# A hybrid decoder step on one core: the order of work in the softmax of the prompt's latent attention

## The chip, the cores and the metric

The kernel runs on one core of one Trainium2 chip. The metric is the device time of one execution in microseconds (us). The kernel before took 5193.56 us, the median of 3 runs (5190.1 to 5200.91).

## The reference, cut to what matters

One step of a one-layer decoder for a prompt of 512 tokens and a sample group of 8 x 4 tokens, which share the weights: a recurrent branch, multi-head latent attention (MLA) and attention into memory tokens, merged; then a PEER expert layer. The change touches only the MLA of the prompt, 16 heads, causal:

```python
q = jnp.einsum('bsc,chd->bshd', rmsnorm(qa, g_q_a), w_q_b)
q_nope, q_pe = q[..., :NOPE_DIM], rope(q[..., NOPE_DIM:], q_pos)     # 128 and 64 wide
ckv_new = rmsnorm(kva[..., :KV_LORA], g_kv_a)                        # 256 wide
krope_new = rope(kva[..., KV_LORA:], q_pos)
# per block of 128 queries, per head:
s = (q_abs . ckv + q_pe . kpe) * (NOPE_DIM + ROPE_DIM) ** -0.5
s = jnp.where(k_pos <= pos, s, -inf)
o = softmax(s) @ ckv            # then the value half of w_kv_b
```

All data are float32.

## The kernel before

One program of five engines' instruction streams, ordered by hand; engines wait for each other's semaphores with constant or loop-dependent counts. There is no planner for this part. The prompt's projections come first, then the memory attention, then the prompt's MLA, the sample's MLA over its gathered pages, the merges, and PEER, which takes most of the time.

The prompt's MLA is a loop of 4 with two rounds inside (L722 to L784 on TensorE, L1158 to L1184 on ScalarE, L1501 to L1537 on VectorE). A round `n` does two heads, `e` = 0 and 1. It has these steps:

- TensorE makes three query products of 4 x 2 matmuls each (`cols`, L571; into the bank pairs 0/1, 2/3 and 6/7; the first has the nope part of one head, the second that of the other, the third the rotary part of both), then the keys of both heads (L737, banks 0 and 1), the swapped rotary part (L571), the values (L744, banks 2 and 3), and the sample's absorbed queries (L749, bank 4). ScalarE copies query, key and value products out of PSUM (L1165, L1167, L1168); VectorE applies the rotation (L1508 to L1511).
- The softmax part goes in steps `u`, one for each block of 128 queries of each head, 8 in all; block `t` = `u % 4` has `(t + 1) * 128` keys. Scores (L763, L764) go to bank `u % 3`. VectorE adds the causal mask (L1529) and takes the negative maximum (L1470, L1471). ScalarE takes the exponential and its sum into `pbuf` (L1127). VectorE normalises (L1474, L1475). TensorE transposes the probabilities in blocks of 128 (L774) into bank 5 or 6, ScalarE copies them to `pT` (L1183), and after the fourth block of a head TensorE multiplies with the values into bank 7 (PV, L782), which VectorE copies to `omla` (L1537, semaphore `mla_out`).
- TensorE transposes step `u - 2` after the scores of step `u`: a lag of two. ScalarE's stream has the same lag: exp of `u`, then the copy of `u - 2`. VectorE normalises with a lag of one.
- `spin(bank, n)` (L566) issues `n` fillers: matmuls of a matrix of ones with 512 columns of `hT`, into a bank that nobody reads. Two stand ahead of the softmax part, one ahead of each of the first six transposes, two ahead of each of the last two, and one ahead of each PV product.
- Before the three query products of a round TensorE waits until VectorE has stored the last output of the round before (`mla_out`, L728).

In the trace one float32 matmul is two records. SP loads the weights of a round into two of the five slots of a ring as these come free. When the last round's weight slots are free, GpSimd begins to gather the pages of the first sample sequence (L488 to L498, 16 gathers), which the sample's MLA needs.

Of the kernel before, what the change touches and what calls it, by code (L numbers as in the profile page):

```python
# [25 lines left out]
P = 128  # L26
# [3 lines left out]
SEQ = 512  # L30
NB = 8
NS = 4
SAMP = NB * NS
T = SEQ + SAMP
# [3 lines left out]
ROPE = 64  # L38
# [38 lines left out]
NSCR = 7032  # L77
# [100 lines left out]
def build(nc, A, O):  # L178
    with ExitStack() as ctx:
# [83 lines left out]
        qabs = region(X0 + 4 * T + 1024, 2, NB, 64)  # L263
        assert X0 + 4 * T + 2048 <= OMLA
        vv = region(S0, 4, 256)
        pbuf = region(S0 + 1024, 3, SEQ)
        pT = region(S0 + 1024 + 1536, 4, SEQ)
        qpe = region(S0 + 1024 + 1536 + 2048, NB, 64)[0:ROPE]
        ropt = region(S0 + 1024 + 1536 + 2048 + 512, T)
        assert S0 + 1024 + 1536 + 2048 + 512 + T <= SCR + NSCR  # L270

        qs2 = [region(X0, 3, 64), region(X0 + 2560, 3, 64)]
        ob = region(X0 + 2752, 256)[0:64]
# [279 lines left out]
        def _(pe):  # L553
# [169 lines left out]
            with pe.Fori(0, 4) as i:  # L723
                for e2 in range(2):
                    wa = use("mla", 2 * e2, i)
                    wb = use("mla", 2 * e2 + 1, i)
                    n = i * 2 + e2
                    pe.wait_ge(s("mla_out"), i * 4 + 2 * e2 + 1)  # L728
                    for m in range(3):
                        for k in range(4):  # L730
                            last = cols(pair((0, 1, 3)[m]), wa[:, (4 * m + k) * P:(4 * m + k + 1) * P], proj[:, QA + k, :],
                                        k == 0, k == 3)
                        last.then_inc(s("q_ready"), 1)
# [19 lines left out]
                    spin(5, 2)  # L753
                    pe.wait_ge(s("kv_stored"), n * 2 + 2)
                    pe.wait_ge(s("q_turned"), n * 3 + 3)
                    for u in range(8 + 2):
                        if u < 8:
                            e, t = u // 4, u % 4
                            if u >= 3:
                                pe.wait_ge(s("mla_exp"), n * 8 + u - 2)  # L760
                            bank = u % 3
                            w_ = (t + 1) * P
                            mm(psum[:, bank, 0:w_], qn[:, e, t * P:(t + 1) * P], kn[:, e, 0:w_], start=True, stop=False)  # L763
                            mm(psum[:, bank, 0:w_], qp[64 * e:64 * e + 64, t * P:(t + 1) * P],  # L764
                               proj[64 * e:64 * e + 64, KROPE, 0:w_], start=False, stop=True).then_inc(s("mla_scores"), 1)
                        if u >= 2:
                            q = u - 2
                            e, t = q // 4, q % 4
                            spin(4, 1 if u < 8 else 2)
                            pe.wait_ge(s("mla_probs"), n * 8 + q + 1)  # L770
                            if q >= 2:
                                pe.wait_ge(s("mla_pT"), n * 8 + q - 1)
                            for j in range(t + 1):
                                last = nc.tensor.transpose(psum[:, 5 + q % 2, j * P:(j + 1) * P], pbuf[:, q % 3, j * P:(j + 1) * P], ident)  # L774
                            last.then_inc(s("mla_turned"), 1)
                            if t == 3:
                                spin(4, 1)
                                pe.wait_ge(s("mla_pT"), n * 8 + q + 1)
                                if e == 1:
                                    pe.wait_ge(s("mla_out"), n * 2 + 2)  # L780
                                for j in range(4):
                                    last = mm(psum[:, 7, j * P:SEQ], vv[:, j, e * P:(e + 1) * P], pT[:, j, j * P:SEQ],  # L782
                                              start=(j == 0), stop=(j == 3), skip_group_check=True)
                                last.then_inc(s("mla_pv"), 1)  # L784
# [224 lines left out]
        def _(act):  # L1009
# [148 lines left out]
            with act.Fori(0, 4) as i:  # L1158
                for e2 in range(2):
# [6 lines left out]
                    act.wait_ge(s("kv_ready"), n + 1)  # L1166
                    a_(kn, psum[:, 0:2, :], ACT.Copy).then_inc(s("kv_stored"), 1)  # L1167
                    a_(vv.rearrange("p (a b) n -> p a (b n)", a=2), psum[:, 2:4, :], ACT.Copy).then_inc(s("kv_stored"), 1)  # L1168
                    for u in range(8 + 2):
                        if u < 8:  # L1170
                            t = u % 4
                            act.wait_ge(s("mla_max"), n * 8 + u + 1)
                            if u >= 3:
                                act.wait_ge(s("mla_turned"), n * 8 + u - 2)
                            exp(pbuf[:, u % 3, 0:(t + 1) * P], psum[:, u % 3, 0:(t + 1) * P], v("nm", u % 4, 1), MLA_SCALE,
                                v("sum", u % 4, 1), s("mla_exp"))
                        if u >= 2:
                            q = u - 2
                            t = q % 4
                            act.wait_ge(s("mla_turned"), n * 8 + q + 1)  # L1180
                            if q == 4:
# [143 lines left out]
        def _(dve):  # L1325
# [177 lines left out]
            with dve.Fori(0, 4) as i:  # L1503
                own.enter(i, 2 * (8 + 8 + 8) + 2 * 1)
                for e2 in range(2):
# [18 lines left out]
                    for u in range(9):  # L1524
                        if u < 8:
                            e, t = u // 4, u % 4
                            dve.wait_ge(s("mla_scores"), n * 8 + u + 1)
                            bank = psum[:, u % 3, :]
                            do(V.tensor_tensor(bank[:, t * P:(t + 1) * P], bank[:, t * P:(t + 1) * P], causal, ALU.add))  # L1529
                            neg_max(bank[:, 0:(t + 1) * P], v("nm", u % 4, 1), MLA_SCALE, s("mla_max"))  # L1530
                        if u >= 1:
                            q = u - 1
                            dve.wait_ge(s("mla_exp"), n * 8 + q + 1)
                            normalise(pbuf[:, q % 3, 0:(q % 4 + 1) * P], v("rc", q % 4, 1), v("sum", q % 4, 1), s("mla_probs"))
                    for e in range(2):
                        dve.wait_ge(s("mla_pv"), n * 2 + e + 1)
                        V.tensor_copy(omla[:, ds(i * 4 + e2 * 2 + e, 1), 0:SEQ].squeeze(1), psum[:, 7, :]).then_inc(s("mla_out"), 1)  # L1537
# [472 lines left out]
```

## Time and profile before

| | |
|---|---|
| time, median of 3 | 5193.56 us |
| the profiled execution's own time | 5196.23 us |
| its span | 5194.4 us |
| mean granted TensorE clock | 0.889 |
| TensorE matmul busy | 4054.4 us (78%) |
| VectorE busy | 2797.3 us (54%) |
| GpSimd busy | 1426.3 us (27%) |
| ScalarE busy | 382.5 us (7%) |
| chain that ended last | PE 49%, DMA 23%, DVE 13%, issue 8%, POOL 7%, ACT 1% |
| the filler line L566 in the chain | 2% of the span |

How to read it: the span is that of one profiled execution, from its first to its last instruction. PE is TensorE, PEld its weight loads, DVE VectorE, ACT ScalarE, POOL GpSimd, SP SyncE. The busy share is an average over stages with different limits; which engine bounds the stretch of the change is read from the rows of that stretch. The chain follows back from the last instruction, at each step to what released it.

### The profile page before, as it was taken

Reading aid. Unit: us, or ns where it says so; the run is one execution under the profiler, and the core shown is the slowest. Engines: PE = TensorE matmul, PEld = TensorE weight load, DVE = VectorE, ACT = ScalarE, POOL = GpSimd, SP = SyncE. Lnnn points to the kernel's source line nnn. Section 1 sums busy time; section 2 is a strip of 40 time slices with the busy share of each in tenths; the row PEclk is TensorE's granted clock in tenths of the full one; section 3 lists DMA queues with packets and bytes.
Section 4 is the critical chain, followed back from the end, with each engine's and each line's share of the span. In section 5 each row is a group of like instructions: output and inputs, shape, how many; then the busy total and the mean of one; then the engine's idle time right before and its main releaser. Section 6 shows DMA issues by size and latency. Waiting matters only on the chain.

```text
span 5194.4 us, 39086 instructions
## 1 busy us (share of the span) xinstructions
PE 4054.4 (78%) x14526; PEld 2447.8 (47%) x14526; DVE 2797.3 (54%) x3638; ACT 382.5 (7%) x826; POOL 1426.3 (27%) x1257
## 2 busy tenths in 40 slices
PE   9999999998899999999899796999999990000000
PEld 7888665553389938555555344544443330000000
DVE  3235022321100004777777575688876645699998
ACT  1022012221000001000000001000000000000000
POOL 0000100013400001344455443212122217777533
PEclk9999989999989999999999898999999995555555
DMA  4211520113566645888899996699999987799999
GB/s 156 70 68 65 177 102 25 36 40 122 162 221 243 242 159 198 353 347 355 361 411 412 370 393 264 251 384 393 375 400 419 419 338 249 271 406 410 417 422 377
DMA packets 234203, 1413.25 MB, mean 272 GB/s; under 512 B 34704, under 2 KB 35536, under 8 KB 86416
## 3 DMA queue, kind: packets, MB, share of 16 engines
q0 software_dynamic: 138960, 916.70, 44.9%
q1 hardware_dynamic: 81984, 458.79, 23.5%
q10 hardware_dynamic: 13088, 35.50, 1.8%
q8 instruction: 106, 1.74, 0.1%
q14 instruction: 65, 0.53, 0.0%
HBM read 1385.08 MB, written 25.75 MB: 272 GB/s over the span
## 4 chain that ended last, share of the span: by engine, by line
PE 49%; DMA 23%; DVE 13%; issue 8%; POOL 7%; ACT 1%; DVEq 0%; ACTq 0%; POOLq 0%; another core or an unknown queue 0%
PE psum L571 11%; PE psum L997 10%; DMA arena<-in_v,arena 9%; DMA arena<-in_u_cols 7%; PE psum L866 7%; DVE psum L1865 7%; DMA arena<-in_u,arena 6%; PE psum L975 3%; POOL arena L528 3%; PE psum L566 2%; POOL arena L546 2%; PE psum L905 2%; POOL arena L496 2%; PE psum L928 1%; DVE arena L1755 1%
## 5 line engine op out<-in xcount | busy, mean ns | idle before, releaser
L866 PE MATMUL psum<-arena 128*128 128x160 f32 (+1 forms) x5120 | 1190.0, 396 | 34.2 <-DVE arena L1598 33.4
L1865 DVE SCALAR_TENSOR_TENSOR psum<-arena,psum 128x2048 f32<-128x2048 f32 x381 | 897.4, 2355 | 285.4 <-DMA arena<-in_v,arena 245.9
L866 PEld LDWEIGHTS psum<-arena 128*128 128x128 f32 x5120 | 842.0, 192 | 381.7 <-issue 48.4
L997 PE MATMUL psum<-arena 128*128 128x512 f32 x2048 | 912.0, 599 | 32.9 <-DMA arena<-in_u_cols 28.5
L528 POOL DMA_INDIRECT arena<-in_v,arena x544 | 642.2, 1180 | 840.7 <-DVE psum L1865 362.4
L528 POOL DMA_INDIRECT arena<-in_u,arena x288 | 384.7, 1336 | 1485.7 <-DVE arena L1686 656.5
L997 PEld LDWEIGHTS psum<-arena 128*128 128x128 f32 x2048 | 379.3, 190 | 564.9 <-issue 421.7
L571 PE MATMUL psum<-arena 128*128 128x272 f32 x2432 | 561.6, 393 | 8.4 <-DVE arena L1537 6.5
L571 PEld LDWEIGHTS psum<-arena 128*128 128x128 f32 x2432 | 462.3, 190 | 105.1 <-DVE arena L1537 7.8
L1755 DVE SCALAR_TENSOR_TENSOR arena<-arena,pages 128x2048 f32<-128x2048 f32 x128 | 301.1, 2353 | 102.9 <-DMA arena<-in_v,arena 99.3
L1720 DVE CUSTOM_DVE_ANT_0 arena<-arena 128x2048 f32<-128x2048 f32 x128 | 291.3, 2293 | 87.4 <-DMA arena<-in_u,arena 86.7
L1837 DVE CUSTOM_DVE_ANT_0 arena<-arena,psum 128x2048 f32<-128x2048 f32 x128 | 288.4, 2285 | 88.2 <-DMA arena<-in_u,arena 87.5
L546 POOL DMA_INDIRECT arena<-products,arena x256 | 246.7, 964 | 137.8 <-issue 136.9
L489 POOL COPY stage_idx<-pages 128x16 uint32 x8 | 1.6, 195 | 724.2 <-PE psum L749 587.8
L566 PE MATMUL psum<-arena,ones 128*128 128x512 f32 (+1 forms) x416 | 197.4, 592 | 0.0
L952 PE MATMUL psum<-arena 128*128 128x512 f32 x384 | 167.4, 599 | 35.4 <-DVE arena L1598 35.4
L975 PE MATMUL psum<-arena 128*128 128x384 f32 x512 | 167.7, 486 | 1.0 <-ACT arena L1281 1.0
L483 POOL TENSOR_TENSOR arena<-arena 128x544 f32<-128x544 f32 x16 | 21.7, 1393 | 511.1 <-PE psum L571 511.1
L1365 DVE TENSOR_TENSOR arena<-psum,arena 128x544 f32<-128x544 f32 x31 | 22.5, 724 | 252.4 <-PE psum L571 251.7
L1470 DVE TENSOR_REDUCE vec<-psum 128x1 f32<-128x128 f32 (+2 forms) x88 | 41.6, 473 | 186.5 <-PE psum L669 179.5
L952 PEld LDWEIGHTS psum<-arena 128*128 128x128 f32 x384 | 73.8, 193 | 128.8 <-issue 92.8
L496 POOL DMA_INDIRECT arena<-in_pool_rows,stage_idx x128 | 121.8, 952 | 45.2 <-issue 38.3
(276 smaller groups left out, 3033.7 us busy)
## 6 DMA issues: line engine op xcount, KB each, us to landing
arena<-in_w_merge SPq DMA_DIRECT2D x160, 1024.0 KB
arena<-in_u_cols SPq DMA_DIRECT2D x256, 512.0 KB
arena<-in_w_out SPq DMA_DIRECT2D x32, 1024.0 KB
arena<-in_w_query SPq DMA_DIRECT2D x32, 1024.0 KB
arena<-in_w_proj SPq DMA_DIRECT2D x31, 1024.0 KB, 4.9
products<-arena ACTq DMA_DIRECT2D x32, 512.0 KB, 12.3
arena<-in_v,arena POOLq DMA_INDIRECT x544
arena<-in_w_mem_k SPq DMA_DIRECT2D x8, 1024.0 KB, 6.2
```

Of the source, the lines that this page charges most:

```text
L528: pool.indirect_dma_start(row, None, A[table], bass.IndirectOffsetOnAxis(ap=idx[:, r:r + 1], axis=0))\
L546: pool.indirect_dma_start(dense_acts[:, e:e + 1], None, products, bass.IndirectOffsetOnAxis(ap=elem_idx[:, e // 128, e % 128:e % 128 + 1], ...
L566: mm(psum[:, bank, 512 - width:512], ones[:, :], hT[:, 0, 0:width], start=True, stop=True)
L571: last = mm(out[:, a, :], w, rhs[:, a * HALF:(a + 1) * HALF], start=start, stop=stop)
L866: last = mm(out, w[:, (off + k) * P:(off + k + 1) * P], src[:, k0 + k, lo:hi], start=(k == 0), stop=(k == n - 1))
L952: last = mm(psum[:, 3 * (n % 2) + t, :], merged_b[:, 4 * q + k, t * P:(t + 1) * P], w[:, k, :], start=(q == 0 and k == 0), stop=(q == 3 an ...
L975: last = mm(psum[:, u % 2, 0:B_N], w[:, k * P:(k + 1) * P], hfT_b[:, k, :], start=(k == 0), stop=(k == KD - 1))
L997: last = mm(psum[:, 4 + DENSE * (b % 2) + t, :], hfT_b[:, k0 + k, t * P:(t + 1) * P], u_tiles[n % 4][:, k, :], start=(k0 + k == 0), stop=( ...
L1720: V.tensor_tensor_reduce(row, row, h, 1.0, 0.0, ALU.mult, ALU.add, out).then_inc(s("rows_used"), 1)
L1755: V.scalar_tensor_tensor(lone, row, atmp_3[:, r:r + 1], lone, ALU.mult, ALU.add).then_inc(s("rows_used"), 1)
L1837: V.tensor_tensor_reduce(four(row), four(row), acc[0], 1.0, 0.0, ALU.mult, ALU.add, acts_2[:, r:r + 1]).then_inc(s("rows_used"), 1)
L1865: V.scalar_tensor_tensor(a, four(row), atmp_b[:, t, r:r + 1], a if r else four(x1_b[:, t, :]), ALU.mult, ALU.add).then_inc(s("rows_used"), 1)
```

## The change

Scores rotate over four banks instead of three, `pbuf` has four buffers instead of three, and the lag between scores and transposes is three steps on TensorE and ScalarE. The waits that guard the rotation move by one accordingly. Fillers stand only ahead of the last three transposes, one each, and, as before, ahead of PV and of the softmax part. TensorE's wait for the last output of the round before stands ahead of the third query product instead of the first. `qpe` and `ropt` and `pT` get other addresses in the same memory. VectorE's lag is the same. The core of the diff:

```diff
-        pbuf = region(S0 + 1024, 3, SEQ)
-        pT = region(S0 + 1024 + 1536, 4, SEQ)
-        qpe = region(S0 + 1024 + 1536 + 2048, NB, 64)[0:ROPE]
-        ropt = region(S0 + 1024 + 1536 + 2048 + 512, T)
+        pbuf = region(S0 + 1024, 4, SEQ)
+        pT = region(S0 + 1024 + 2048, 4, SEQ)
+        qpe = region(X0 + 4 * T + 2048, NB, 64)[0:ROPE]
+        ropt = region(S0 + 1024 + 2048 + 2048, T)
...
-                    pe.wait_ge(s("mla_out"), i * 4 + 2 * e2 + 1)
                     for m in range(3):
+                        if m == 2:
+                            pe.wait_ge(s("mla_out"), i * 4 + 2 * e2 + 1)
...
-                    for u in range(8 + 2):
+                    for u in range(8 + 3):
                         if u < 8:
                             e, t = u // 4, u % 4
-                            if u >= 3:
-                                pe.wait_ge(s("mla_exp"), n * 8 + u - 2)
-                            bank = u % 3
+                            if u >= 4:
+                                pe.wait_ge(s("mla_exp"), n * 8 + u - 3)
+                            bank = u % 4
...
-                        if u >= 2:
-                            q = u - 2
+                        if u >= 3:
+                            q = u - 3
                             e, t = q // 4, q % 4
-                            spin(4, 1 if u < 8 else 2)
+                            if u >= 8:
+                                spin(4, 1)
                             pe.wait_ge(s("mla_probs"), n * 8 + q + 1)
...
-                    for u in range(8 + 2):
+                    for u in range(8 + 3):
                         if u < 8:
                             t = u % 4
                             act.wait_ge(s("mla_max"), n * 8 + u + 1)
-                            if u >= 3:
-                                act.wait_ge(s("mla_turned"), n * 8 + u - 2)
+                            if u >= 4:
+                                act.wait_ge(s("mla_turned"), n * 8 + u - 3)
...
-                        if u >= 2:
-                            q = u - 2
+                        if u >= 3:
+                            q = u - 3
```

## Rows read from the trace of the kernel before

**Rows 1.** The chain that ended last, 700 to 1200 us, shares by line.

```profile
by line: PE psum L566 22.9%; PE psum L571 19.8%; PE psum L764 9.4%; PE psum L782 7.6%; PE psum L763 7.5%; PE psum L744 5.5%; PE psum L737 5.5%; PE psum L774 3.5%; issue 3.0%; PE psum L714 2.6%; PE psum L811 1.5%; PE psum L705 1.5%; PE psum 
```

**Rows 2.** Windows: length, busy us (instructions) of each engine, granted clock, DMA share, GB/s.

```profile
895.00:946.00 51.00, 50.44 (x180) 29.83 (x180) 15.29 (x52) 11.77 (x29) 0.00 (x0) 1.00 0.09 31
1101.00:1163.00 62.00, 52.13 (x180) 30.45 (x180) 15.40 (x51) 11.82 (x29) 15.64 (x17) 0.92 0.28 85
```

**Rows 3.** Waits of TensorE from 792 to 1100 us: us in total, times, longest.

```profile
PE psum L571 <- DVE arena L1537: 5.6, 6, 0.9
```

**Rows 4.** Timeline, TensorE, one round: start, us, line, shapes, records, idle before.

```profile
916.88 0.38 PE L763 MATMUL psum<-arena 128*128 128x128 f32 x2
...
917.61 0.70 PE L763 MATMUL psum<-arena 128*128 128x256 f32 x2
...
918.87 0.91 PE L763 MATMUL psum<-arena 128*128 128x384 f32 x2
...
920.55 1.12 PE L566 MATMUL psum<-arena,ones 128*128 128x512 f32 x2
921.51 0.27 PE L774 MATMUL psum<-cst,arena 128*128 128x128 f32 x1
921.62 1.02 PE L763 MATMUL psum<-arena 128*128 128x512 f32 x2
...
923.63 1.12 PE L566 MATMUL psum<-arena,ones 128*128 128x512 f32 x2
...
930.25 2.41 PE L782 MATMUL psum<-arena 128*128 128x512 f32 x8
932.49 0.81 PE L763 MATMUL psum<-arena 128*128 128x384 f32 x2
...
938.33 1.88 PE L566 MATMUL psum<-arena,ones 128*128 128x512 f32 x4
940.05 0.49 PE L774 MATMUL psum<-cst,arena 128*128 128x128 f32 x3
...
943.40 2.41 PE L782 MATMUL psum<-arena 128*128 128x512 f32 x8
946.74 11.27 PE L571 MATMUL psum<-arena 128*128 128x272 f32 x48 [0.93 <-DVE arena L1537]
```

**Rows 5.** The same round's timeline, VectorE.

```profile
920.03 0.29 DVE L1475 TENSOR_SCALAR arena<-arena,vec 128x128 f32<-128x128 f32 x1
920.66 0.30 DVE L1529 TENSOR_TENSOR psum<-psum,cst 128x128 f32<-128x128 f32 x1 [0.34 <-PE psum L764]
...
921.85 0.35 DVE L1475 TENSOR_SCALAR arena<-arena,vec 128x256 f32<-128x256 f32 x1
923.74 0.30 DVE L1529 TENSOR_TENSOR psum<-psum,cst 128x128 f32<-128x128 f32 x1 [1.54 <-PE psum L764]
...
925.06 0.42 DVE L1475 TENSOR_SCALAR arena<-arena,vec 128x384 f32<-128x384 f32 x1
```

**Rows 6.** The same round's timeline, ScalarE.

```profile
924.99 0.69 ACT L1127 ACTIVATE arena<-psum,vec 128x512 f32<-128x512 f32 x1 [2.37 <-DVE vec L1471]
...
929.58 0.60 ACT L1183 ACTIVATE arena<-psum 128x512 f32<-128x512 f32 x1
```

**Rows 7.** Timeline of the last round, each of the three engines' stall.

```profile
1139.25 0.30 DVE L1529 TENSOR_TENSOR psum<-psum,cst 128x128 f32<-128x128 f32 x1 [6.71 <-remote]
...
1144.88 0.60 ACT L1183 ACTIVATE arena<-psum 128x512 f32<-128x512 f32 x1 [4.08 <-remote]
...
1145.53 4.08 PE L782 MATMUL psum<-arena 128*128 128x512 f32 x8 [9.64 <-ACT arena L1183]
```

**Rows 8.** Windows elsewhere in the kernel.

```profile
1205.00:1210.00 5.00, 3.09 (x8) 0.65 (x6) 1.22 (x1) 0.00 (x0) 3.78 (x5) 1.00 0.84 259
...
710.00:715.00 5.00, 5.00 (x27) 2.94 (x27) 1.03 (x5) 0.56 (x2) 0.00 (x0) 0.50 0.00 0
```

**Rows 9.** Timeline, TensorE, ahead of 710 us.

```profile
706.33 4.75 PE L714 MATMUL psum<-arena 128*128 128x4 f32 x32
```

More of the change, by code:

```diff
@@ L265, in build @@
         vv = region(S0, 4, 256)
-        pbuf = region(S0 + 1024, 3, SEQ)
-        pT = region(S0 + 1024 + 1536, 4, SEQ)
-        qpe = region(S0 + 1024 + 1536 + 2048, NB, 64)[0:ROPE]
-        ropt = region(S0 + 1024 + 1536 + 2048 + 512, T)
-        assert S0 + 1024 + 1536 + 2048 + 512 + T <= SCR + NSCR
+        pbuf = region(S0 + 1024, 4, SEQ)
+        pT = region(S0 + 1024 + 2048, 4, SEQ)
+        qpe = region(X0 + 4 * T + 2048, NB, 64)[0:ROPE]
+        ropt = region(S0 + 1024 + 2048 + 2048, T)
+        assert S0 + 1024 + 2048 + 2048 + T <= SCR + NSCR and X0 + 4 * T + 2048 + 512 <= OMLA
         qs2 = [region(X0, 3, 64), region(X0 + 2560, 3, 64)]
@@ L773, in _ @@
                             for j in range(t + 1):
-                                last = nc.tensor.transpose(psum[:, 5 + q % 2, j * P:(j + 1) * P], pbuf[:, q % 3, j * P:(j + 1) * P], ident)
+                                last = nc.tensor.transpose(psum[:, 5 + q % 2, j * P:(j + 1) * P], pbuf[:, q % 4, j * P:(j + 1) * P], ident)
                             last.then_inc(s("mla_turned"), 1)
@@ L1172, in _ @@
                             act.wait_ge(s("mla_max"), n * 8 + u + 1)
-                            if u >= 3:
-                                act.wait_ge(s("mla_turned"), n * 8 + u - 2)
-                            exp(pbuf[:, u % 3, 0:(t + 1) * P], psum[:, u % 3, 0:(t + 1) * P], v("nm", u % 4, 1), MLA_SCALE,
+                            if u >= 4:
+                                act.wait_ge(s("mla_turned"), n * 8 + u - 3)
+                            exp(pbuf[:, u % 4, 0:(t + 1) * P], psum[:, u % 4, 0:(t + 1) * P], v("nm", u % 4, 1), MLA_SCALE,
                                 v("sum", u % 4, 1), s("mla_exp"))
-                        if u >= 2:
-                            q = u - 2
+                        if u >= 3:
+                            q = u - 3
                             t = q % 4
@@ L1527, in _ @@
                             dve.wait_ge(s("mla_scores"), n * 8 + u + 1)
-                            bank = psum[:, u % 3, :]
+                            bank = psum[:, u % 4, :]
                             do(V.tensor_tensor(bank[:, t * P:(t + 1) * P], bank[:, t * P:(t + 1) * P], causal, ALU.add))
@@ L1533, in _ @@
                             dve.wait_ge(s("mla_exp"), n * 8 + q + 1)
-                            normalise(pbuf[:, q % 3, 0:(q % 4 + 1) * P], v("rc", q % 4, 1), v("sum", q % 4, 1), s("mla_probs"))
+                            normalise(pbuf[:, q % 4, 0:(q % 4 + 1) * P], v("rc", q % 4, 1), v("sum", q % 4, 1), s("mla_probs"))
                     for e in range(2):
```

## The prediction, made before the change was run

> **What bounds the kernel now.** I read the chain of waits over the stretch around the change first. The chain from 700 to 1200 us lies on TensorE almost throughout, and its largest line is L566, the filler matmuls, with 22.9% [rows 1]. In this stretch the chain runs through work whose result nobody reads.
>
> The windows say the same. The eight rounds of the prompt's MLA end at about 1163 us. A round takes 51 us, its TensorE time is 50.44 us of 51.00, VectorE has 15.29 and ScalarE 11.77, DMA is at 0.09, and the granted clock is 1.00 [rows 2]. So a microsecond taken off TensorE in a round is a microsecond off the kernel, as long as no wait takes its place. Everything after MLA starts on MLA's results (the sample's attention, then merges and PEER, whose weight loads begin only after the sample's last result), so I count the rest as shifted, not changed. The last round is another case: 62 us, with one TensorE wait of 9.64 us [rows 2, 7].
>
> The list of waits gives TensorE one regular wait in the rounds: 0.9 us, once a round, for VectorE's copy at L1537, six of them in the six rounds seen [rows 3]. The timeline of one round (rows 4; all full rounds have this pattern) shows where the time goes: its softmax part runs from 916.88 to the end of the last PV product at 945.8 (943.40 + 2.41), 28.8 us without a TensorE gap; the next round begins at 946.74; the other 22 us of a round are query, key and value products.
>
> **Part 1, the fillers.** Before, one filler stands ahead of each of the first six transposes and two ahead of each of the last two, ten in all, and one more ahead of each PV product. After, there is one ahead of each of the last three transposes, and the two ahead of PV stay. Removed: 10 - 3 = 7 a round. One filler is two matmul records. Two fillers take 1.72 us (938.33 to 940.05), so one is 0.86 us; after a score product it takes 0.96 us (920.55 to 921.51), and I count those 0.10 us as the score product's tail that stays [rows 4]. 7 x 0.86 = 6.02 us a round off TensorE's own work.
>
> **Part 2, the lag: what is late next.** The fillers gave ScalarE and VectorE time; now the third step of lag and the fourth bank must. I place the new order on a line with 0 at the first score product, with durations from rows 4 to 6. Scores 0 and 1 take 2.0 us together (916.88 to 918.87; 0.73 and 1.26), score 2 1.68 and score 3 2.01 us (921.62 to 923.63), a transpose 0.11 us a block of 128 (921.51 to 921.62), a PV product 2.24 us (930.25 to 932.49) [rows 4]. VectorE's step 2 lasts 1.54 us (920.66 to 922.20), step 3 1.74 us (923.74 to 925.48), and ScalarE's exp starts 1.25 us into it (924.99); the smaller ones take some 1.3 to 1.4 [rows 5]. ScalarE's exp of 512 takes 0.69 us, to which I add 0.1 for the read-out of its sum, its copy of 512 turned probabilities 0.60 us; smaller ones go down to about half [rows 6].
>
> - Scores 0 to 3 end at 5.7 without a gap. Probabilities 0 were ready 3.4 us after the first score's start (920.03 + 0.29 [rows 5]), so transpose 0 doesn't wait. Score 4 needs exp 0 (2.2): no wait.
> - Score 4, transpose 1, score 5, transpose 2, score 6, transpose 3 follow at 6.6, 6.8, 8.0, 8.5, 10.1, 10.6. VectorE goes through its steps 3, 4, 5 as they come and has probabilities 2 at 7.4 and 3 at 8.8: in time, with 0.7 us or more to spare. The copy of turned block 0 now stands behind exp 3 and ends at 7.9, transpose 2 wants its bank at 8.1: just in time.
> - The filler ends at 11.5. PV needs the copy of turned block 3, and in ScalarE's new order this stands behind exp 6, not exp 5. Score 6 ends at 10.1, its maximum is there at 11.3, exp 6 ends at 12.0, the copy at 12.6. **TensorE waits 1.1 us here.** This is the one real new wait.
> - PV, score 7 (end at 16.9), transpose 4, filler, transpose 5, filler: 19.0. Transpose 6 wants the bank of turned block 4, whose copy stands behind exp 7 (ends 19.0), so it starts at about 19.3: 0.25 us more. Transpose 7 and the last filler end at 21.7, the last copy at 21.6; the output of the first head must have been copied out of bank 7, which VectorE does after normalisation 7, at about 20.4. No wait. PV ends at 24.0.
>
> Laid out the same way, the order of before ends at 28.8, as the trace has it. So the softmax part goes from 28.8 to 24.0: 6.0 us removed, 1.35 given back, **4.7 us** a round. Bounds: 6.0 if the two waits cost nothing; 3.0 if they are twice as long and every transpose also waits a little (eight times 0.2 us: the distance from the end of a score to VectorE's start is 0.1 us, 923.63 to 923.74 [rows 4, 5]).
>
> **Part 3, the wait at the third query product.** It removes the 0.93 us in front of each round's first product [rows 3, 4]. The first two products take a third of 11.27 us each [rows 4], write banks 0 to 3, and by then VectorE's copy (0.69 us) is long over, so the moved wait costs nothing. Queued behind it are the third product and the key products; nothing comes late. ScalarE still waits for the same copy before it stores the first product, which ends 3.7 us in. Seven boundaries between eight rounds: 7 x 0.93 = **6.5 us**. The wait after the last round stays.
>
> **Part 4, buffers.** A fourth pbuf and other addresses for pbuf, pT, qpe and ropt change neither count nor size of any instruction, nor a DMA. Cost 0; I take 1 us to either side for what an address could do, about a hundredth of VectorE's 8 x 15.29 us [rows 2].
>
> **Part 5, the last round.** Its stall comes while GpSimd issues sixteen page gathers, begun when the round's last weight tile is free; VectorE shows 6.71 us and ScalarE 4.08 us idle before instructions whose inputs were there, released by something that the trace can't name, and TensorE waits 9.64 us and runs the next PV at half clock (4.08 us against 2.41) [rows 4, 7]. The gathers start at the same place of the round after the change, so I let VectorE come free at the same point, 1139.25 on the old scale, and ScalarE at 1144.9. In the new order exp 6 and copy 3 follow that: PV at 1146.5 instead of 1145.53. On the line above, 12.6 to 24.0 is 11.4 us from there, and a PV at half clock adds 1.9: the round ends at 1159.8, where it now ends at 1162.8. The last round gains **3 us**; bounds 0 (ScalarE's stall moves behind exp 6) and 15 (no stall: 4.7 and the 10.6 us by which this round is longer than the others).
>
> **Sum.** 7 x 4.7 + 6.5 + 3 = 42.4 us, against the profiled execution's 5196.2 us (span 5194.4 and 1.8 around it): 5153.8 us. That execution lies 2.7 us above the median of 5193.6; I state the prediction from the median: 5193.6 - 42.4 = **5151 us**. Ends of the terms: 7 x 3.0 + 6.5 + 0 = 27.5 (5166) and 7 x 6.0 + 6.5 + 15 = 63.5 (5130).
>
> **The clock, weighed.** TensorE is now 3% idle in a round where it had been full. In the trace the clock stays at 1.00 in 1205 to 1210 us with 3.09 of 5 us busy, so an idle microsecond does not lower it at once. But it was at 0.50 in 710 to 715 us with TensorE busy 5.00 of 5 us [rows 8], behind 32 matmuls of 4 columns [rows 9]: busy time alone doesn't hold the clock, and the fillers are 512 columns wide. For this kernel the first argument weighs more, because the scores, transposes and PV that remain are 128 to 512 columns wide. The Trainium skill (TensorE: Matmul & The Clock Gate, "A second HAM failure mode: psum-queue depth-cycling") says that short idle times between groups of matmuls, in a kernel that cycles through PSUM banks, can be enough for the clock to swing between its two levels. By that rule this change, more cycling and less filler, would be a loss; the trace of before has no such swing in the rounds.
>
> **Rivals.**
> - *The clock gives way* (the other side). Place: the softmax part of each round. Its TensorE work after the change is some 22.5 us a round at 2.4 GHz and would be twice that at 1.2 GHz (PV: 4.08 against 2.41 as recorded). Over 8 rounds a share f of it at the lower level costs 180 x f. It decides from f = 42/180 = 0.24; with f a third, 60 us: 5211 us; with all of it 5331 us. For it: rows 8 and 9. Against it: 1.00 in the rounds, the 22 us of dense products in each, and that scores 0 to 2 run without filler already, at full clock. Chance 0.09.
> - *Waits take the fillers' place.* Each step still lasts what ScalarE and VectorE need, and only part 3 and a few tenths a round stay: 5193.6 - 6.5 - 8 x 1.5 = 5175 us, or 5187 with nothing in the softmax. Against it: VectorE and ScalarE together are busy 27 of 51 us, and probabilities were ready over 1 us before their transposes. Chance 0.08, of which 0.04 within 0.2%.
> - *The last round's stall goes or halves*, because the stretch in which it falls is shorter or differently ordered: 6 to 12 us more than the sum, 5139 to 5145 us. The cause of the stall isn't in the rows. Chance 0.10.
> - *The forecast*, 27 to 50 us gained: 0.73.
>
> **How the numbers follow.** About 0.2%, 10 us, is what a measurement of this kernel tells from no change. Faster by more: 0.73 + 0.10 + 0.04 = 0.87; within: 0.04; slower: 0.09. The range goes from 5137, into the case without a stall, to 5169, just beyond the lower end of the terms, and leaves out the clock case and most of the waits' case.
>
> **What would show it.** The record of L566 in the rounds drops from 28 records to 14; TensorE's wait for L1537 at L571 is gone; a new TensorE wait of about 1 us for ScalarE's L1183 ahead of the first PV of each round; the round's period goes from 51.4 to 45.7 us; granted clock 1.00 in the full rounds; the stretch after MLA as long as before. A granted clock under 0.9 in the rounds, or TensorE waits ahead of most transposes, would make the prediction wrong.

## The result, and the profile after

The changed kernel takes 5144.24 us, the median of 4 runs (5135.76 to 5147.55); the kernel before took 5191.83 us (4 runs, 5187.19 to 5200.91). The ratio is 0.9904, 95% interval [0.9885, 0.9923]: 50 us faster, give or take 10. The forecast was 5151 us, 42.4 us less than before; it is right in sign and, for the full rounds, in mechanism.

The chain of the same stretch, 700 to 1200 us, by line:

```profile
by line: PE psum L571 19.7%; PE psum L765 9.1%; issue 8.5%; PE psum L784 7.9%; PE psum L764 7.7%; PE psum L566 7.0%; PE psum L745 5.5%; PE psum L738 5.5%; POOL arena L496 4.7%; PE psum L776 3.1%; PE psum L714 2.4%; PE psum L813 2.2%; DVE ve
```

The fillers (L566) have gone from 22.9% [rows 1] to 7.0%; query and key products (L571) now lead. The page gathers (POOL L496, 4.7%) and most of the larger share of "issue" (8.5%, was 3.0%) don't come from the full rounds: MLA ends 46 us earlier here, so the same stretch reaches 46 us further into the sample's MLA, and the last round's stall (below) holds one piece of 8 us. In the six full rounds alone "issue" is 3.0% of the chain and was 0.2%; that part belongs to the two new waits.

Windows of a full round and of the last (length, busy us of each engine with its instructions, granted clock, DMA share, GB/s):

```profile
876.00:921.00 45.00, 43.86 (x165) 26.60 (x164) 15.47 (x51) 11.60 (x29) 0.00 (x0) 1.00 0.11 35
1058.00:1117.00 59.00, 46.96 (x167) 28.22 (x166) 15.70 (x52) 11.82 (x29) 15.64 (x17) 0.88 0.29 89
```

Against [rows 2] the full round has lost 6 us, and its clock, the share of the full 2.4 GHz that TensorE was granted, is still 1.00; TensorE is busy 43.86 of 45 us. Its waits in six full rounds (us in total, times, longest):

```profile
PE psum L784 <- ACT arena L1185: 5.5, 6, 0.9
PE psum L776 <- ACT arena L1185: 1.1, 6, 0.2
```

The wait of [rows 3] is gone, and the two that the prediction named are there, once a round each, for ScalarE's copy L1185 (L1183 before). One full round on TensorE (start, us, line, shapes, records, idle before):

```profile
897.44 0.38 PE L764 MATMUL psum<-arena 128*128 128x128 f32 x2
...
907.60 0.66 PE L776 MATMUL psum<-cst,arena 128*128 128x128 f32 x4
908.09 1.02 PE L566 MATMUL psum<-arena,ones 128*128 128x512 f32 x2
910.03 2.42 PE L784 MATMUL psum<-arena 128*128 128x512 f32 x8 [0.92 <-ACT arena L1185]
912.29 1.02 PE L764 MATMUL psum<-arena 128*128 128x512 f32 x2
...
915.54 1.02 PE L566 MATMUL psum<-arena,ones 128*128 128x512 f32 x2
916.74 0.52 PE L776 MATMUL psum<-cst,arena 128*128 128x128 f32 x3 [0.18 <-ACT arena L1185]
...
918.39 1.02 PE L566 MATMUL psum<-arena,ones 128*128 128x512 f32 x2
919.25 2.41 PE L784 MATMUL psum<-arena 128*128 128x512 f32 x8
921.50 3.83 PE L571 MATMUL psum<-arena 128*128 128x272 f32 x16
```

The softmax part begins at 897.44 and its last PV at 919.25: 21.81 us, where it was 26.52 (916.88 to 943.40 [rows 4]), 4.71 us less. The filler ahead of the first PV starts at 908.09 and would be done 0.86 us later, at 908.95; PV starts at 910.03: 1.08 us of wait (the list counts 0.92, from the filler's modelled end). ScalarE shows why: the copy that PV needs stands behind the exp of step 6.

```profile
908.82 0.58 ACT L1129 ACTIVATE arena<-psum,vec 128x384 f32<-128x384 f32 x1 [0.61 <-DVE vec L1473]
...
909.39 0.59 ACT L1185 ACTIVATE arena<-psum 128x512 f32<-128x512 f32 x1
```

Ahead of transpose 6 it is 916.74 - (915.54 + 0.86) = 0.34 us. And the next round's products begin 2.25 us after the last PV's start (921.50), not 3.34 (943.40 to 946.74 [rows 4]). The round's period, from first product to first product, is 45.48 us (876.02 to 921.50) and was 51.37 (895.37 to 946.74), 5.89 us less.

The last round's stall is in this execution too, on VectorE, ScalarE and TensorE:

```profile
1099.83 0.30 DVE L1531 TENSOR_TENSOR psum<-psum,cst 128x128 f32<-128x128 f32 x1 [10.30 <-remote]
```

```profile
1092.80 0.49 ACT L1185 ACTIVATE arena<-psum 128x384 f32<-128x384 f32 x1 [3.06 <-remote]
...
1101.99 0.60 ACT L1185 ACTIVATE arena<-psum 128x512 f32<-128x512 f32 x1 [0.38 <-remote]
```

```profile
1102.64 4.63 PE L784 MATMUL psum<-arena 128*128 128x512 f32 x8 [11.62 <-ACT arena L1185]
...
1114.40 2.41 PE L784 MATMUL psum<-arena 128*128 128x512 f32 x8
```

VectorE stands for 10.30 us, ScalarE for 3.06 us at one copy, TensorE for 11.62 us, and again the next PV runs at half clock (4.63 us, where the second PV takes 2.41). "remote" means that the trace doesn't name the releaser. The round takes 59.81 us instead of 62.84.

### The profile page after: what moved, and what is told of

The parts are those of the page before. It is cut to its first block, busy times and chain, and to the rows that moved or that the text cites. A ratio compares the mean times of both kernels' runs of the same rounds, so it can differ in the third digit from the quotient of the medians.

```text
span 5134.0 us, 38854 instructions
## 1 busy us (share of the span) xinstructions
PE 3999.1 (78%) x14414; PEld 2424.2 (47%) x14414; DVE 2795.3 (54%) x3638; ACT 381.6 (7%) x826; POOL 1442.6 (28%) x1257
## 4 chain that ended last, share of the span: by engine, by line
PE 47%; DMA 24%; DVE 10%; issue 9%; POOL 9%; ACT 1%; ACTq 0%; DVEq 0%; POOLq 0%; another core or an unknown queue 0%
PE psum L571 11%; PE psum L999 10%; DMA arena<-in_v,arena 9%; DMA arena<-in_u_cols 8%; PE psum L868 7%; DMA arena<-in_u,arena 6%; POOL arena L528 4%; DVE psum L1867 4%; PE psum L977 3%; POOL arena L546 3%; PE psum L907 2%; POOL arena L496 2%; PE psum L930 1%; DVE arena L1757 1%; DVE arena L1722 1%
## 5 line engine op out<-in xcount | busy, mean ns | idle before, releaser
L528 POOL DMA_INDIRECT arena<-in_u,arena x288 | 403.8, 1402 | 1459.9 <-DVE arena L1688 656.2
L571 PE MATMUL psum<-arena 128*128 128x272 f32 x2432 | 562.5, 394 | 1.8 <-DVE arena L1501 0.9
L571 PEld LDWEIGHTS psum<-arena 128*128 128x128 f32 x2432 | 463.4, 191 | 97.7 <-issue 2.2
L566 PE MATMUL psum<-arena,ones 128*128 128x512 f32 (+1 forms) x304 | 135.6, 567 | 0.0
L496 POOL DMA_INDIRECT arena<-in_pool_rows,stage_idx x128 | 121.9, 952 | 45.2 <-issue 38.3
```

The source lines that it names most:

```text
L496: pool.indirect_dma_start(page_buf[:, pg, :], None, A["pool_rows"], bass.IndirectOffsetOnAxis(ap=stage_idx[:, pg:pg + 1], axis=0))\
L528: pool.indirect_dma_start(row, None, A[table], bass.IndirectOffsetOnAxis(ap=idx[:, r:r + 1], axis=0))\
L571: last = mm(out[:, a, :], w, rhs[:, a * HALF:(a + 1) * HALF], start=start, stop=stop)
```

## The experiments

A table first. "Full round" is the period of rounds 2 to 7, "MLA" the stretch from the first query product to the first instruction after the last round, "rest" what comes behind it. Times are medians; the kernel before was run again beside each group.

| kernel | time, ratio to before [95%] | full round | last round | MLA | rest |
|---|---|---|---|---|---|
| before | 5191.8 | 51.37 | 62.84 | 423.8 | 4030.7 |
| before, again | 5173.5 (one run) | 51.37 | 51.37 | 412.6 | 4022.1 |
| changed | 5144.2, 0.9904 [0.9885, 0.9923] | 45.48 | 59.81 | 381.2 | 4016.3 |
| changed, again | 5142.7 (one run) | 45.48 | 46.57 | 366.5 | 4034.7 |
| e1 wait only | 5171.9, 0.998 [0.9967, 0.9993] | 50.18 | 51.27 | 405.3 | 4027.3 |
| e2 fillers only | 5144.1, 0.9932 [0.991, 0.9954] | 46.87 | 49.22 | 381.0 | 4019.2 |
| e3 lag only | 5182.6, 1.0005 [0.9995, 1.0015] | 51.56 | 51.56 | 414.1 | 4025.2 |
| e4 copy first | 5115.6, 0.9879 [0.9855, 0.9903] | 43.93 | 45.02 | 355.5 | 4020.9 |
| e5 no filler | 5205.1, 1.0002 [0.9986, 1.0018] | 47.91 to 54.56 | 62.62 | 440.7 | 4027.7 |
| e6 gathers after the round | 5147.4, 0.9918 [0.9895, 0.9941] | 45.48 | 46.56 | 366.7 | 4034.1 |
| e7 gathers at the first PV | 5134.9, 0.9888 [0.9868, 0.9908] | 45.48 | 46.57 | 366.7 | 4028.9 |
| e8 e4 and e7 | 5124.9, 0.9865 [0.9841, 0.9889] | 43.93 | 45.02 | 355.3 | 4025.3 |
| e9 copy first, fewer fillers | 5122.5, 0.9889 [0.9871, 0.9908] | 43.60 to 44.97 | 45.98 | 360.5 | 4026.3 |
| e10 no filler in the softmax | 5152.9, 0.9954 [0.9939, 0.9968] | 47.38 to 48.11 | 48.48 | 386.0 | 4023.8 |

One thing has to be read from it before anything else: "rest" runs the same instructions in all of them and differs by up to 18 us between single executions, and by 18 us between two of the same kernel. A whole time can't settle a microsecond; the period of a full round can: it repeats to 0.01 us in every kernel but e5, e9 and e10 (and in e2 one of the full rounds, the second, took 49.20), where the clock fell within rounds, as is shown below.

**e1, the wait alone.** The kernel before with

```diff
-                    pe.wait_ge(s("mla_out"), i * 4 + 2 * e2 + 1)
                     for m in range(3):
+                        if m == 2:
+                            pe.wait_ge(s("mla_out"), i * 4 + 2 * e2 + 1)
```

> The kernel before with only the wait for the last output moved to the third query product. My theory (the gain is TensorE's own work and its one regular wait, step by step): the 0.93 us in front of each round's first product goes, the period of a full round falls from 51.37 to 50.44 us, the softmax part stays at 28.8 us, the time falls by 6.5 us. Rival (the wait was cover for something, ScalarE's stores say): the 0.93 us turns up again ahead of the key products, the period stays at 51.4, no change.

Measured: period 50.18 us, 1.19 less, not 0.93; the whole time is 10 us less (by the interval 4 to 17), where 6.5 were expected. The timeline of TensorE:

```profile
889.97 2.41 PE L783 MATMUL psum<-arena 128*128 128x512 f32 x8
892.22 11.16 PE L571 MATMUL psum<-arena 128*128 128x272 f32 x48
```

From the last PV's start the products now begin after 2.25 us instead of 3.34, 1.09 less, and the 48 product records take 11.16 where they took 11.27. The trace's idle of 0.93 us counts from the modelled end of the last matmul; the time until the next one could start, had it been free, begins 0.16 us earlier, and a stream that starts behind an idle engine takes 0.1 us longer. The rival, that the wait turns up elsewhere, is out.

**e2, the fillers alone.** The kernel before, lag and banks as they were:

```diff
-                            spin(4, 1 if u < 8 else 2)
+                            if q >= 5:
+                                spin(4, 1)
```

> The kernel before with the same seven fillers a round taken out, at the old lag of two, three banks and three pbufs, old wait. Theory A (TensorE's own work sets the round; the lag matters little): laid out with the same durations, new waits are 0.75 us for probabilities 2 and 0.86 us for the copy ahead of the first PV, the softmax part goes from 28.8 to 24.4 us and the period from 51.4 to 47.0; 31 us in seven rounds, about 3 in the last: 5158 us where before has 5192. Rival B (the third step of lag and the fourth bank are what makes the fillers removable): every transpose waits for its probabilities, the period stays at 49 or above and the gain under 18 us, or the clock falls in the softmax part.

Measured: period 46.87 us, 4.50 less, 5144.1 us, by the ratio 35 us less than before, where 34 were expected. Waits of TensorE in four full rounds:

```profile
PE psum L571 <- DVE arena L1538: 3.7, 4, 0.9
PE psum L775 <- DVE arena L1476: 3.3, 4, 0.8
PE psum L783 <- ACT arena L1184: 2.7, 4, 0.7
```

Beside the old wait at L571 they are the two forecast ones, for probabilities (0.8 a round) and ahead of the first PV (0.7), and nothing else. Rival B fails on the period and the gain: the fillers come out at the old lag. But in one point it is half right, the clock. In two of the eight rounds, the second (49.20 us) and the last (49.22), the clock fell right behind the wait for probabilities; in the second round:

```profile
817.55 0.55 PE L775 MATMUL psum<-cst,arena 128*128 128x128 f32 x3 [0.82 <-DVE arena L1476]
```

```profile
816.00:818.00 2.00, 1.18 (x9) 0.87 (x9) 1.86 (x7) 1.00 (x3) 0.00 (x0) 1.00 0.00 0
818.00:820.00 2.00, 2.00 (x5) 0.71 (x4) 0.73 (x4) 0.89 (x4) 0.00 (x0) 0.50 0.00 0
820.00:823.00 3.00, 3.00 (x8) 1.87 (x8) 1.24 (x5) 1.05 (x3) 0.00 (x0) 0.50 0.00 0
```

Each such fall costs about 2.3 us. With the lag of three and the same fillers (the changed kernel, its repetition, e6 and e7) no full round shows one.

**e3, the lag alone.** The changed kernel with

```diff
-                            if u >= 8:
-                                spin(4, 1)
+                            spin(4, 1 if q < 6 else 2)
```

and the wait at the first product.

> The changed kernel with the fillers of before (one ahead of transposes 0 to 5, two ahead of 6 and 7) and the wait at the first product again: only lag, banks and buffers are new. Theory A: the softmax part is 28.8 to 29.0 us, period 51.4 to 51.6, the time within 2 us of before. Rival B (the lag brings time by itself): period 50 or less, gain of 10 us or more.

Measured: period 51.56, 0.19 more than before, TensorE busy in 50.62 of 51 us:

```profile
896.00:947.00 51.00, 50.62 (x180) 29.83 (x180) 15.09 (x52) 11.77 (x29) 0.00 (x0) 1.00 0.09 31
```

e1, e2 and e3 now split the 5.89 us of an undisturbed round: wait 1.19, fillers 4.50, and what the lag and the banks add to these two, 0.20. Three of the edits of the change (lag, fourth bank, fourth buffer) so bring 1.6 us of 50 in waits; besides, in the one execution of e2 that was profiled, their absence let the clock fall twice, about 4.7 us together.

**e4, what is left.** The changed kernel with the two blocks of ScalarE's step exchanged:

```diff
                     for u in range(8 + 3):
+                        if u >= 3:
+                            q = u - 3
+                            ... the copy of q
                         if u < 8:
                             ... exp of u
-                        if u >= 3:
-                            q = u - 3
-                            ... the copy of q
```

> The changed kernel with ScalarE's order within a step turned: the copy of turned block u-3 first, then exp u. Theory A: the waits of TensorE ahead of the first PV (measured 0.92 plus what is ahead of it, 1.08 us in all) and ahead of transpose 6 (0.34 us) exist because the copies stand behind exp 6 and exp 7; both go, the period falls from 45.5 to 44.1 us, the time by about 10 us against the changed kernel (5134 us). Rival: exp u is delayed by the copy and TensorE waits for probabilities instead; the period stays within 0.3 us of 45.5.

Measured: period 43.93, 1.55 less; TensorE waits for nothing in a full round:

```profile
874.00:917.00 43.00, 43.00 (x162) 26.32 (x161) 15.46 (x51) 11.85 (x29) 0.00 (x0) 1.00 0.11 37
```

So both new waits came from the order of ScalarE's stream, and from nothing that an engine lacked in time. With the lag of three the copy can go first, since its transpose is issued right behind the scores whose maximum the exp still waits for; the change left that unused. Whether the turned order would also do at the old lag was not run, so that it is the lag which allows it is not shown. This version is faster than before (0.9879 [0.9855, 0.9903]). Against the changed kernel the whole times don't settle it, since the two intervals overlap, but the MLA does: it is 11.0 us shorter (366.5 to 355.5, two executions without a stall), 1.55 us in each of seven rounds.

**e5, no filler at all.** The changed kernel without the three ahead of transposes, the two ahead of PV and the two ahead of the softmax part.

> The changed kernel without any filler in the prompt's MLA: the three ahead of the last transposes, the two ahead of PV and the two ahead of the softmax part are out. Theory A (the clock holds at these idle shares, waits take over): laid out with the same durations TensorE waits 2.0 us ahead of the first PV, 1.5 ahead of transpose 6, 0.5 and 0.2 ahead of 7, 0.75 ahead of the last PV; the softmax part is 23.2 us instead of 24.0, and the start of the softmax part waits for ScalarE's copies of keys and values at about where the two fillers ended; the period is 44.6 to 45.5, the gain over the changed kernel 0 to 7 us, the granted clock 1.00. Rival (the clock gives way): the clock falls below 0.95 in the full rounds and the period goes above 46 us; at 0.5 in a third of the softmax part it would be some 50 us a round.

Measured: 5205.1 us (ten executions, 5177.11 to 5209.56), the ratio to before 1.0002 [0.9986, 1.0018]: the whole gain is gone, though no filler is run, where the changed kernel has 7 a round and the kernel before 14. Windows through one of its rounds (the first column is the stretch, the figure behind the busy times the granted clock):

```profile
872.00:875.00 3.00, 2.55 (x10) 1.48 (x10) 1.31 (x7) 0.78 (x3) 0.00 (x0) 0.98 0.60 175
875.00:880.00 5.00, 5.00 (x7) 1.50 (x6) 2.33 (x9) 1.24 (x4) 0.00 (x0) 0.50 0.00 0
880.00:885.00 5.00, 5.00 (x13) 2.42 (x11) 2.84 (x10) 1.68 (x6) 0.00 (x0) 0.50 0.00 0
885.00:890.00 5.00, 5.00 (x13) 2.25 (x11) 1.87 (x7) 0.95 (x3) 0.00 (x0) 0.50 0.00 0
890.00:895.00 5.00, 3.68 (x7) 1.70 (x6) 0.80 (x4) 1.16 (x3) 0.00 (x0) 0.50 0.00 0
895.00:900.00 5.00, 3.28 (x12) 1.41 (x10) 1.74 (x6) 0.91 (x4) 0.00 (x0) 0.97 0.00 0
900.00:906.00 6.00, 5.14 (x16) 3.01 (x17) 1.15 (x3) 1.39 (x4) 0.00 (x0) 0.72 0.00 0
```

and TensorE's idle times in it:

```profile
872.45 0.46 PE L763 MATMUL psum<-arena 128*128 128x128 f32 x2 [1.30 <-ACT arena L1166]
...
891.66 4.23 PE L780 MATMUL psum<-arena 128*128 128x512 f32 x8 [1.32 <-ACT arena L1181]
...
900.18 1.12 PE L773 MATMUL psum<-cst,arena 128*128 128x128 f32 x7 [1.89 <-ACT arena L1181]
```

At 872.45 it had waited 1.30 us for ScalarE's copy of keys and values, where the two fillers stood, just behind the narrow products of 32 columns (L750). From 875 us on the clock is 0.50 in spite of a TensorE that is busy without a gap, and stays there until the next PV has run. Theory A is wrong, the rival right; the price is 9 us a round. In two of the eight rounds (the fifth, 47.91 us, behind 1.30 us, and the last, behind 1.27 us) the same wait did not lower it, and only waits further on did. The Trainium skill (TensorE: Matmul & The Clock Gate, "A second HAM failure mode: psum-queue depth-cycling") says of a bf16 kernel that short idle times between groups of matmuls, as it cycles through PSUM banks, can make the clock swing between its levels: by this kernel the trace agrees, 0.50 behind 1.30 us, and by two rounds of e2, behind 0.82 us; by the changed kernel, with one more bank in the cycle and idle times of 1.08 and 0.34 us, it doesn't.

**e10, which fillers hold it.** The two ahead of the softmax part are back, the five inside it stay out.

> The changed kernel without the five fillers inside the softmax part, with the two ahead of it. In the kernel without any filler the clock fell in two places: at the third score, behind a wait of 1.3 us that stands where these two were, and at the PV products, behind waits of 1.8 us. Theory: the two fillers ahead hold the clock through the scores and transposes of the first head; the waits ahead of PV then lower it for the PV products: period 47 to 49 us, granted clock about 0.93 to 0.96. Rival 1 (either place alone is harmless): clock 1.00, period 44.8 us. Rival 2 (only the sum of fillers counts): clock 0.8, period 52 us or more.

```profile
885.00:919.00 34.00, 32.68 (x130) 21.51 (x129) 12.58 (x43) 8.85 (x23) 0.00 (x0) 1.00 0.14 46
919.00:923.00 4.00, 3.50 (x6) 1.89 (x7) 0.00 (x0) 0.45 (x1) 0.00 (x0) 0.57 0.00 0
923.00:929.00 6.00, 3.92 (x17) 1.75 (x16) 2.89 (x8) 1.86 (x6) 0.00 (x0) 1.00 0.00 0
929.00:933.00 4.00, 3.50 (x6) 1.82 (x7) 0.00 (x0) 0.45 (x1) 0.00 (x0) 0.57 0.00 0
```

Measured: full rounds of 47.38 to 48.11 us. Scores and transposes run at 1.00; each PV, behind a wait of 1.77 us or of 1.90 and 0.69, runs mostly at 0.50. The theory's numbers (47 to 49 us, about 0.93 to 0.96) hold. Granted over a whole round it is 0.93. The fillers inside the softmax part are needed too: leaving out 5 of them, 4.3 us of TensorE's work, makes the round 2.3 us longer (45.48 to 47.8 on average).

**e9, the three ahead of the transposes.** e4 without them.

> The changed kernel with ScalarE's copy ahead of its exp and without the three fillers ahead of the last transposes; those ahead of PV and of the softmax part stay. If the clock holds: TensorE waits about 1.5 us ahead of transpose 6 and 0.7 ahead of 7, the period is 43.4 to 43.6 us instead of 43.93, 3 us better than with the three fillers, so they were nearly all wait already. Rival (the clock gives way, as it did when all fillers went): the granted clock in the full rounds is under 1.00, a PV product at half clock costs 1.8 us and the period is 45 us or more.

```profile
833.00:877.00 44.00, 42.54 (x159) 26.43 (x158) 15.23 (x51) 11.85 (x29) 0.00 (x0) 0.96 0.11 36
877.00:921.00 44.00, 42.18 (x165) 26.43 (x164) 15.46 (x51) 11.85 (x29) 0.00 (x0) 1.00 0.11 36
```

```profile
PE psum L774 <- DVE arena L1475: 13.6, 14, 1.4
```

Measured: both theories in turn. The waits are there (13.6 us in 14, up to 1.4 us; 1.36 and 0.46 us ahead of the last two transposes of a round). In two full rounds the clock held and the period is 43.60 us, as laid out; in four others, with the same waits, it fell for a while and the period is 44.64 to 44.97. On average 44.4, worse than 43.93 with the fillers in.

**e6, e7 and e8, the last round.** The changed kernel (e8: e4) with one line ahead of GpSimd's loop over the sample's sequences:

```diff
             pool.wait_ge(ring_used, PLAN["end"]["base"] + RING)
+            pool.wait_ge(s("mla_out"), 17)         # e6
+            pool.wait_ge(s("mla_pv"), 15)          # e7, e8
```

> The changed kernel with GpSimd's first page gathers held back until the last round's last output is stored. Theory C (the last round's stall comes from the gathers' traffic: ScalarE and VectorE stand before instructions whose inputs are there as long as the gathers run): the last round is as long as the others, 45.5 us plus nothing, the 11.6 us wait at PV is gone; the sample's MLA then waits for its first pages, which take 23 us from the first gather, with 5 us of that covered by what stands ahead: the stage up to the second sequence's pages is longer by 14 to 20 us, so the whole is 0 to 8 us slower than the changed kernel. Rival D (the stall belongs to the end of the loop or to the code, not to the gathers): the last round keeps a wait of about 10 us, and the whole is 15 to 20 us slower.

> The changed kernel with the first page gathers held back until the first PV product of the last round has ended, some 12 us later than now if there is no stall. Theory C: until that PV the round runs as the others do; the stall moves behind it, and I can't say from the traces whether any engine needs what is delayed in the 9 us that are left: gain over the changed kernel between 2 and 11 us if not, 0 if the stall comes anyway, since the pages land 23 us after the first gather and that is only 2 to 4 us later than the sample's first page product wants them. Rival D: last round's wait of about 10 us at the PV stays, no gain, 2 to 4 us slower.

> The changed kernel with both: ScalarE's copy ahead of its exp in each step, and the gathers held back until the last round's first PV. If both theories hold the gains add: about 10 us from the order and 2 to 11 us from the gathers, 12 to 21 us under the changed kernel, 60 to 69 us under the kernel before. If the order brings nothing and the stall comes anyway: within 3 us of the changed kernel.

Measured: none of the three has the stall in its last round; these rounds are 46.56, 46.57 and 45.02 us, and e8 is no better than e4 (MLA 355.3 and 355.5 us), which had no stall to lose. e6 pays with a later sample stage (300.3 us from the end of MLA to the first product of its results, 289.9 in e7 and in the changed kernel run again), e7 pays nothing. Taken alone, that would confirm theory C. It doesn't, because of the next two.

**The two kernels again.**

> The kernel before, unchanged, profiled once more: does the last round's stall (9.6 us ahead of its first PV) belong to the kernel or to the execution? If to the kernel (its code, its place): last round 62.8 us again. If to the execution: any value from 51.6 us up; the three variants in which the gathers start as before and no stall showed speak for this.

> The changed kernel, unchanged, profiled once more, the same question: 59.8 us for the last round again, or 46.6 us without a stall. The full rounds at 45.48 us in any case.

The last round of before and of the changed kernel, in windows of these executions:

```profile
1098.00:1149.00 51.00, 50.44 (x180) 29.83 (x180) 15.67 (x52) 11.76 (x29) 15.60 (x17) 1.00 0.34 103
```

```profile
1057.00:1107.00 50.00, 47.52 (x178) 28.58 (x176) 16.97 (x55) 12.28 (x31) 15.60 (x17) 1.00 0.35 105
```

No stall, in either: 51.37 and 46.57 us, with the same 17 instructions on GpSimd. The stall belongs to the execution. In the last round it showed in three of the eleven profiled executions in which the gathers start early (before, changed, e5); the 2.3 us by which e2's last round is longer are the clock's. That it was in none of three with held gathers would happen by chance about four times in ten (8/11 cubed). Nor is it gone where they are held. Behind MLA, in the sample's part, VectorE stands in the same way in e7 (first line) and twice in e6 (the other two):

```profile
1117.96 1.22 DVE L1563 TENSOR_REDUCE vec<-psum 64x1 f32<-64x1024 f32 x1 [12.48 <-remote]
```

```profile
1197.12 1.22 DVE L1563 TENSOR_REDUCE vec<-psum 64x1 f32<-64x1024 f32 x1 [13.61 <-remote]
1338.79 1.22 DVE L1563 TENSOR_REDUCE vec<-psum 64x1 f32<-64x1024 f32 x1 [15.01 <-remote]
```

In e7 the product that it reads ended 1.9 us before, in e6 4.3 and 5.7 us before; most of each wait is one that it has anyway. So five of fourteen executions have such a stall, and holding the gathers back moves its place. Every wait of this kind in the fourteen traces falls in or right behind a series of sixteen gathers: VectorE comes free 0.3 to 2.8 us after the last of them in five cases, in before 3 us ahead of its end, with ScalarE 2.6 us behind it. That the gathers are needed for it is likely by this, and not shown; what exactly the engines stand for stays open.

## Why the prediction was right

- *TensorE bounds the rounds, and what is taken off it is gained.* Shown by e2: 6.0 us of fillers out, 4.5 us gained, the rest in two named waits.
- *Part 1 and 2, 4.7 us a round.* Measured 4.71 (26.52 to 21.81). The two waits were laid out at 1.1 and 0.25 us and are 1.08 and 0.34. The line-up from single durations was good to 0.1 us because every engine's order is fixed and all durations repeat. (The part before is 28.9 us by 945.8 less 916.88 and 28.8 with a PV of 2.24 us; both orders are counted the second way, so the difference stands.)
- *Part 3, 0.93 us a boundary.* A term mis-sized: 1.19 by e1. It was read off the idle column, which begins at a modelled end. 7 x 0.26 = 1.8 us too little, and just what the forecast of the period is off: 45.7 against 45.48.
- *Part 4, nothing.* e3 contains the addresses and is at 0.19 us a round; its softmax part is 0.18 us longer (917.70 to 944.40 against 26.52), by a wait ahead of the first PV. What the addresses alone do was not run; by this it is next to nothing.
- *Part 5, the last round, 3 us.* Measured 3.03 (62.84 to 59.81) in the two executions that have the stall. That is luck. VectorE was to come free 38.4 us into the round, as before, and ScalarE's copy to follow 5.6 us later, with PV 1 us later than before; in fact VectorE came free at 41.9 us (1099.83), the copy 2.2 us behind it, and PV began where it had, 44.7 us into the round. The 3 us were all gained behind PV. And the premise, that the stall is the kernel's, was wrong: without it the round goes from 51.37 to 46.57, 4.8 us. The upper bound of 15 us was short as well: from a round with the stall to one without it is 62.84 to 46.57, 16.3 us. (The 10.6 us compare a round without its closing wait with a period that has one; like for like it is 11.5.)
- *The sum.* 42.4 us forecast for MLA; 423.8 to 381.2 = 42.6 with the stall on both sides, 412.6 to 366.5 = 46.1 without it. That the first pair meets the sum to 0.2 us is partly luck: seven rounds of 5.89 and 3.03 would be 44.3, but the first round gained only 4.23 (52.78 to 48.55). In the changed kernel's execution the clock was at 0.50 from 736 to 740 us, where its products began, and its first 48 product records took 14.23 us, against 12.67 in the execution of before; in the repeated pair, with 12.72 in the changed kernel, the first round gained 5.93. The median moved by 47.6 and the profiled pair by 60.4: the difference lies 3.3 us ahead of MLA and 14.4 us behind it ("rest" 4030.7 and 4016.3), where the repeated pair has 12.6 us the other way. It is scatter, not the change.
- *The clock.* The rival was given 0.09 and did not occur; e5 and two rounds of e2 show that it was near. The reason that I gave, wide matmuls and a full engine in the products, is not enough: e5 has both. What held the clock were the fillers that the change left in: e5 against e10 shows it for the two ahead of the softmax part, e10 for the five inside it, and e9, with ScalarE's order turned, for the three ahead of the transposes. At the old lag they were not enough in two rounds of e2, so the new lag, which the forecast counted in waits only, seems to have a part in it; that rests on one profiled execution.
- *Waits take the fillers' place.* 1.4 of 6.0 us a round, as laid out, no more.

## What to carry to other kernels

Write down each engine's order with its durations and walk it before changing a lag or a bank count: here that gave the round's period to 0.3 us (45.7 against 45.48, 47.0 against 46.87 in e2, 44.1 against 43.93 in e4), and it told ahead of e3 that the deeper lag alone gains nothing, and ahead of e4 what turning ScalarE's stream would bring. Fillers are of two kinds, those that only pass time on an engine that then has no wait, and those that stand in a wait and hold the clock; take out the first, and try the second one place at a time with the granted clock in view. And where single executions scatter by more than the effect, read the period of a repeated round, and profile the unchanged kernel twice before explaining anything that occurs once, and search the whole trace for it before calling it gone.

## What the runs showed of the hardware that was not expected

- A TensorE that is busy without a gap ran at half clock for 15 us and more (875 to 890 us in e5), after an idle time of only 1.30 us behind narrow products; idle times of 1.08 us in the full rounds of the changed kernel never lowered it, one of 0.82 us did in two of e2's eight rounds, and those of 1.36 and 0.46 us in e9 did in four of six full rounds. The length of the idle time alone doesn't tell.
- A stall, in five of fourteen executions, around the sixteen page gathers that GpSimd issues: VectorE, and in the last round ScalarE too, stand ahead of instructions whose inputs are there, and the trace names no releaser. In the last round TensorE then waits 9.6 to 13.8 us; behind MLA little of it shows.
- The same instructions behind MLA take 4016 to 4035 us, by execution; between two of the changed kernel the difference is 18.4 us.
